# Second block's attention: gates two to a step at first, the dilated projection inside the last steps, weight splits in halves

## The chip, the cores and the metric

The kernel runs on one core of one Trainium2 chip. The metric is the device time of one execution in microseconds (us). Before the change it is 2328.41 us, the median of 3 runs (2326.83 to 2332.44).

## The reference, cut to what matters

Two transformer blocks follow each other, on 256 tokens of width 1024. The change lies in the second block's token mixer, between its input projection and its mixture of experts. There are three dilated groups of four heads (12 in all), and 16 heads with a window of 128 and a sink. Both attentions are projected, each is multiplied by the sigmoid of a gate, and the sum goes through an output projection:

```python
def token_mixer(x, w_in, sinks, w_proj_a, w_proj_b, w_out, slopes):
    h = jnp.einsum('bsd,dc->bsc', x, w_in)
    a_q, a_k, a_v, b_q, b_k, b_v, g_a, g_b = jnp.split(h, SPLIT_POINTS, axis=-1)
    ...
    out_a = dilated_attention(a_q, a_k, a_v, slopes_a)
    out_b = swa_sink_attention(b_q, b_k, b_v, slopes_b, sinks.reshape(SWA_KV_HEADS, SWA_REP))
    merged = (jax.nn.sigmoid(g_a) * jnp.einsum('bsc,cd->bsd', out_a, w_proj_a)
              + jax.nn.sigmoid(g_b) * jnp.einsum('bsc,cd->bsd', out_b, w_proj_b))
    return jnp.einsum('bsd,de->bse', merged, w_out)
```

`out_a` is 256 wide and `out_b` 1024 wide. Then come a layer norm, a router that picks 4 of 32 experts for each token, and the experts, whose weights (12 MB for each) are all read from HBM.

## The kernel before

Each engine runs its own program in order, written as one Python function for each: `pe`, `dve`, `act`, `pool` and `sync` (the queue that issues the weight loads). They meet through semaphores.

**Weights.** A weight tile `t` is loaded by `sync` into one of three raw slots (`t % 3`), after the last use of tile `t - 3` (`wlast[t - 3]`). Matrix products are done in three passes, so the tile is split in two parts of less precision: ScalarE writes the high part in `hi(t, p0, p1)`, piece by piece of 1024 columns, and VectorE subtracts it from the raw tile in `lo(t, p0, p1)`. Before its first piece `hi` waits for the load and for the last use of the tile that held the high slot before (`wlast[hprev[t]]`). A full tile has four pieces, `W_PA` has two. TensorE waits for all pieces of a tile (`s_wlo`, `cum[t + 1]`) before it uses it. `rows(name, ...)` makes one output bank of 128 x 256 with `mm3`, three matmuls for each of 8 contraction slices (24 matmuls; 6 for `pa`, which has two slices).

**Tiles of this part.** `W_GATE` to `W_GATE + 3` are the gates (four output rows of each, so gate row `d` of 0 to 15 needs tile `W_GATE + d // 4`), `W_PA` is the dilated projection, `W_PB` and `W_PB + 1` the window projection, `W_PB + 2` and `W_PB + 3` (the last, `NW - 2` and `NW - 1`) the output projection.

**Banks.** `take` gives the eight PSUM banks in turn, leaving out those that are held, and makes TensorE wait until the bank's earlier content has been emptied. The turn is fixed when the program is built.

**Steps.** The attention is a software pipeline of 15 steps on TensorE. In step s it makes the scores `S2` of head-units 2s and 2s+1 (s below 12), one gate row, the transposes `T2` of the units of step s-2, and the output product of the units of step s-3: `oa` (dilated, steps 3 to 6) or `ob[s - 7]` (window, steps 7 to 14). VectorE in step s takes bias and row maximum of the new scores, divides those of step s-1, and empties `oa` (steps 5, 7) or `ob[s - 8]`; then it runs the split. ScalarE in step s takes the exponentials, the high part of `oa` or `ob[s - 8]`, copies `T2` and the gate row out of PSUM, then runs its side of the split. GpSimd prepares the biases.

Splits stand in steps 1, 5 and 9 (four pieces each: `W_GATE + 1`, `+ 2`, `+ 3`) and in step 12 (`W_PA`). Gate row 15 stands behind the pairs of step 14. After the steps TensorE makes the eight `pa`, then the eight `pb`, then the eight `wx` (output projection, interleaved with the sums of the layer norm). ScalarE takes the two sigmoids after the steps, splits `W_PB`, copies the experts' biases (`bias_`), then `W_PB + 1` and the rest. VectorE multiplies `pa` with the gates, then goes over d from 0 to 7: multiply `pb[d]`, add, subtract the high part of ScalarE (lines 1357, 1359, 1362), with the splits of `W_PB + 1` and `W_PB + 2` before d = 0 and d = 4 and that of `W_PB + 3` behind d = 7.

**The queue.** `sync` waits for the last `ob`, loads the first expert tile, then tile `NW - 2` (behind `pa[7]`), another expert tile, then `NW - 1`, and the other experts as slots come free.

Of the kernel before, what the change touches and what calls it, by code (L numbers as in the profile page):

```python
# [12 lines left out]
ACT = mybir.ActivationFunctionType  # L13
AX = mybir.AxisListType.X
ADD, MULT, SUB, MAX, MIN = ALU.add, ALU.mult, ALU.subtract, ALU.max, ALU.min
# [3 lines left out]
KC = D // P  # L19
L = 256  # L20
# [27 lines left out]
def build(nc, a, out):  # L48
# [154 lines left out]
    W_GATE = W_MIX + 9  # L203
# [52 lines left out]
    def filled(name):  # L256
        return done[name]

    def emptied(name):
        b, n = full[name]  # L260
        return s_free[b], n

    def bank(name):
        return ps[full[name][0]]
# [4 lines left out]
    def freesem(name):  # L269
        return s_free[full[name][0]]  # L270
# [56 lines left out]
    def rows_used(kind, u):  # L327

        if kind == "na":
            return filled(("O", u // 4)) if u % 4 == 3 else (s_no, 3 * (u // 4) + u % 4 + 1)  # L330
        if u >= 8:
            return filled(("ob", (u - 8) // 2))
        return filled(("oa", u // 4)) if u // 2 % 2 else (s_no, 24 + u // 4 + 1)

    def mix_unit(u):

# [37 lines left out]
    def pe(e):  # L374
# [27 lines left out]
        def rows(name, T, t, c, i=0, pair_=None, ready=None, ks=KC):  # L402

            pt = take(e, name)
            w = wpair(t, i)
            for k in range(ks):
                if ready:
                    ready(k)
                r = hpart(k, 0, T) if pair_ is None else half(pair_, slice(None), k)
                ins = mm3(e, pt[:, 0:T], half(w, slice(None), k, slice(P * c, P * c + P)), r, k == 0, k == ks - 1)  # L410
            ins.then_inc(fullsem(name))
# [290 lines left out]
        def gate(i, d):  # L702
            t = W_GATE + 2 * i + d // 4
            if d % 4 == 0:
                e.wait_ge(s_wlo, cum[t + 1])
            rows(("gt", i, d), L, t, d % 4, pair_=xs_)
            wlast[t] = filled(("gt", i, d))


        for step in range(15):  # L710
            if step < 4:
                c, n = step // 2, step % 2
                pts = [take(e, ("S2", 2 * step + z)) for z in range(2)]
                if n == 0:
                    for g in range(3):
                        e.wait_ge(*emptied(("aq", 2 * g + c)))
                        e.wait_ge(*emptied(("ak", 2 * g + c)))
                for g, o, ks in ((0, slice(0, L), slice(0, L)), (1, slice(L, L + P), slice(P * n, P * n + P)),
                                 (2, slice(L + P, L + 2 * P), slice(P * n, P * n + P))):
                    for z, pt in enumerate(pts):  # L720
                        r = slice(64 * z, 64 * z + 64)
                        ins = e.matmul(pt[:, o], aq[r, 2 * g + c, P * n:P * n + P], ak[r, 2 * g + c, ks], start=True,
                                       stop=True)
                        if g == 2:
                            ins.then_inc(fullsem(("S2", 2 * step + z)))
            elif step < 12:
                c = step - 4
                pts = [take(e, ("S2", 2 * step + z)) for z in range(2)]
                if c == 0:
                    for g in range(2):  # L730
                        e.wait_ge(*emptied(("bk", g)))
                e.wait_ge(*emptied(("bq", c)))
                for n, (at, w) in enumerate(((0, P), (P, L))):
                    for z, pt in enumerate(pts):
                        r = slice(64 * z, 64 * z + 64)
                        ins = e.matmul(pt[:, at:at + w], bq[r, c, P * n:P * n + P], bk[r, c // 4, 0:w], start=True,
                                       stop=True)
                        if n:
                            ins.then_inc(fullsem(("S2", 2 * step + z)))
            gate(step // 8, step % 8)  # L740
            if 0 <= step - 2 < 12:
                for u in (2 * step - 4, 2 * step - 3):
                    pt = take(e, ("T2", u))
                    e.wait_ge(s_div, 32 + u + 1)
                    for i, at in enumerate((0, P, 2 * P, 3 * P) if u < 8 else (0, P + 1, 2 * P + 1)):
                        ins = e.transpose(pt[:, P * i:P * i + P], at_[:, u % 6, at:at + P], ident)
                    ins.then_inc(fullsem(("T2", u)))
            if 0 <= step - 3 < 4:
                us = 2 * step - 6, 2 * step - 5
                c, n, jj = mix_unit(us[0])  # L750
                pt = bank(("oa", c)) if n else take(e, ("oa", c), hold=True)
                for u in us:
                    e.wait_ge(*emptied(("T2", u)))
                if us[0] == 0:
                    for i in range(2):
                        for m in range(2):
                            e.wait_ge(*emptied(("av", i, m)))
                for i, (g, kb) in enumerate(((0, 0), (0, 1), (1, n), (2, n))):
                    for z, u in enumerate(us):
                        vh = 64 * (4 * g + jj + z)  # L760
                        ins = e.matmul(pt[64 * z:64 * z + 64, P * n:P * n + P], av[:, kb, vh:vh + 64],
                                       turned_[u % 8][:, P * i:P * i + P], start=i == 0, stop=i == 3)
                ins.then_inc(fullsem(("oa", c)) if n else s_no)
            elif step >= 7:
                c = step - 7
                us = 2 * step - 6, 2 * step - 5
                pt = take(e, ("ob", c))
                for u in us:
                    e.wait_ge(*emptied(("T2", u)))
                if c == 0:  # L770
                    e.wait_ge(*emptied(("bv", 0)))
                    e.wait_ge(*emptied(("bv", 1)))
                vh = 64 * (c // 4)
                for n in range(2):
                    for kb in range(n + 1):
                        for z, u in enumerate(us):
                            i = n + kb
                            ins = e.matmul(pt[64 * z:64 * z + 64, P * n:P * n + P], bv[:, kb, vh:vh + 64],
                                           turned_[u % 8][:, P * i:P * i + P], start=kb == 0, stop=kb == n)
                ins.then_inc(fullsem(("ob", c)))  # L780
            if step in (6, 9):
                held.discard(full["oa", step // 3 - 2][0])
            if step == 14:
                gate(1, 7)


        e.wait_ge(s_wlo, cum[W_PA + 1])
        for d in range(KC):
            rows(("pa", d), L, W_PA, d, pair_=oa_, ks=2,
                 ready=(lambda k: e.wait_ge(*emptied(("oa", k)))) if d == 0 else None)  # L790
        wlast[W_PA] = filled(("pa", KC - 1))
        for i in range(2):
            e.wait_ge(s_wlo, cum[W_PB + i + 1])
            for c in range(4):
# [195 lines left out]
    def dve(e):  # L990
# [298 lines left out]
        for step in range(15):  # L1289
# [41 lines left out]
            if step >= 8:  # L1331
# [1 line left out]
                e.wait_ge(s_ahi, 26 + c + 1)  # L1333
                e.tensor_tensor(straight(ob_[1][:, c, :]), shuffled(bank(("ob", c))[:, 0:L]),
                                straight(ob_[0][:, c, :].bitcast(F32)), SUB).then_inc(freesem(("ob", c)), 1)
            if step in (1, 5, 9):
                lo(W_GATE + 1 + step // 4)
            if step == 12:
                lo(W_PA)
        c = KC - 1  # L1340
        e.wait_ge(s_ahi, 26 + KC)
        e.tensor_tensor(straight(ob_[1][:, c, :]), shuffled(bank(("ob", c))[:, 0:L]), straight(ob_[0][:, c, :].bitcast(F32)),
                        SUB).then_inc(freesem(("ob", c)), 1)


        lo(W_PB)
        e.wait_ge(s_sig, 1)
        for d in range(KC):
            e.wait_ge(*filled(("pa", d)))
            e.tensor_tensor(sg[0][:, d, :], sg[0][:, d, :], bank(("pa", d))[:, 0:L], MULT).then_inc(freesem(("pa", d)), 1)  # L1350
        e.wait_ge(s_sig, 2)
        e.wait_ge(*emptied(("pa", KC - 1)))
        for d in range(KC):
# [248 lines left out]
    def act(e):  # L1602
# [209 lines left out]
        def copied(name, dst, n):  # L1812
            e.wait_ge(*filled(name))
            e.copy(dst, bank(name)[:, 0:n]).then_inc(freesem(name), 1)
# [15 lines left out]
        for step in range(16):  # L1830
# [20 lines left out]
            if 0 <= step - 2 < 12:  # L1851
                for u in (2 * step - 4, 2 * step - 3):
# [1 line left out]
                    e.wait_ge(*filled(("T2", u)))  # L1854
                    w = 4 * P if u < 8 else 3 * P
                    e.copy(turned_[u % 8][:, 0:w], bank(("T2", u))[:, 0:w]).then_inc(freesem(("T2", u)), 1)
            if step < 15:
                copied(("gt", step // 8, step % 8), sg[step // 8][:, step % 8, :], L)
            if step == 14:
                copied(("gt", 1, 7), sg[1][:, 7, :], L)  # L1860
            if step in (1, 5, 9):
                hi(W_GATE + 1 + step // 4)
            if step == 12:
                hi(W_PA)
        for i in range(2):
            e.wait_ge(*emptied(("gt", i, KC - 1)))
            e.activation(sg[i], sg[i], ACT.Sigmoid).then_inc(s_sig, 1)


        hi(W_PB)  # L1870
        for i in range(4):
            e.wait_ge(s_late[i], 16)
        e.wait_ge(*filled(("T2", 23)))
# [349 lines left out]
```

## Time and profile before

| what | value |
|---|---|
| median of 3 runs | 2328.41 us (2326.83 to 2332.44) |
| profiled execution, its own time | 2326.65 us |
| its span | 2324.9 us |
| TensorE busy | 2134.9 us (92%) |
| VectorE busy | 846.8 us (36%) |
| ScalarE busy | 567.4 us (24%) |
| GpSimd busy | 71.8 us (3%) |
| HBM read | 591.03 MB, 255 GB/s over the span |

The busy times are averages over stages with different limits. The attention steps of the second block lie between about 1183.7 and 1270.4 us of the span, `pa` and `pb` up to about 1307 us, and the experts from about 1366 us to the end. In rows of a window the columns are the stretch, then for each engine (PE, PEld, DVE, ACT, POOL) its busy time and count, then PEclk (the granted TensorE clock, 1.00 is full), the DMA share, and GB/s.

### The profile page before, as it was taken

The numbers are of one execution on the slowest core, as the hardware profiler recorded it, in microseconds if no ns is written. First come the engines' busy times: TensorE is split into PE (matmuls) and PEld (weight loads), VectorE is DVE, ScalarE is ACT, GpSimd is POOL, SyncE is SP. The second block draws the span as 40 slices with busy tenths as digits, with TensorE's granted clock in tenths as the row PEclk, the third lists the DMA queues.
The fourth block names the chain that finished last, engine by engine and source line by source line (L and its number), as shares of the span: only waits on it lengthen the run. The fifth ranks groups of instructions, "written<-read, shape, count | busy, mean of one in ns | idle before, by whom it ended". The sixth has DMA issues, their size and how long they took to land.

```text
span 2324.9 us, 27020 instructions
## 1 busy us (share of the span) xinstructions
PE 2134.9 (92%) x11534; PEld 1416.6 (61%) x11534; DVE 846.8 (36%) x1505; ACT 567.4 (24%) x935; POOL 71.8 (3%) x118
## 2 busy tenths in 40 slices
PE   6988999999899998999998879998989988989986
PEld 3766888777677568999987843333333333333332
DVE  4344443352584665765455531111111111111113
ACT  3222332332332434543356230000000000000000
POOL 0000000000000130000031000000000000000000
PEclk8999999999999999999999889999999999999998
DMA  9543343422322454545532559999999999999995
GB/s 353 181 145 109 109 144 110 143 90 93 138 98 75 151 170 137 185 150 185 189 120 103 229 205 411 425 428 427 427 427 428 428 428 428 428 427 428 428 427 210
DMA packets 157229, 593.90 MB, mean 255 GB/s; under 512 B 6416, under 2 KB 79120, under 8 KB 132016
## 3 DMA queue, kind: packets, MB, share of 16 engines
q1 hardware_dynamic: 155104, 589.53, 64.1%
q10 hardware_dynamic: 2000, 2.57, 0.4%
q8 instruction: 94, 1.54, 0.3%
q14 instruction: 31, 0.25, 0.0%
HBM read 591.03 MB, written 1.05 MB: 255 GB/s over the span
## 4 chain that ended last, share of the span: by engine, by line
PE 76%; DMA 13%; DVE 6%; ACT 3%; issue 2%; SPq 1%; ACTq 0%; POOL 0%; DVEq 0%; POOLq 0%
PE ps L897 21%; PE ps L279 13%; PE ps L280 13%; PE ps L281 13%; DMA ring<-in_w_up_dram 12%; PE ps L866 3%; PE ps L883 3%; DVE wr L1004 2%; PE ps L382 2%; PE ps L637 1%; PE ps L616 1%; DMA ring<-in_even_w_in_dram 1%; PE ps L623 1%; SPq L2037 1%; PE ps L396 1%
## 5 line engine op out<-in xcount | busy, mean ns | idle before, releaser
L897 PE MATMUL ps<-ring,big 128*64 128x512 f32 x3072 | 693.4, 607 | 81.3 <-DMA ring<-in_w_up_dram 51.5
L897 PEld LDWEIGHTS ps<-ring,big 128*64 128x64 f32 x3072 | 250.5, 140 | 495.4 <-issue 483.8
L279 PE MATMUL ps<-h_hi,wr 128*128 128x512 f32 (+1 forms) x960 | 341.2, 355 | 29.5 <-DVE h_lo L1056 25.2
L1004 DVE TENSOR_TENSOR wr<-ring,wr 128x1024 fp32r<-128x1024 f32 (+1 forms) x248 | 285.5, 1210 | 140.4 <-ACT wr L1611 140.3
L280 PE MATMUL ps<-h_lo,wr 128*128 128x512 f32 (+1 forms) x960 | 333.2, 347 | 0.0
L281 PE MATMUL ps<-h_hi,wr 128*128 128x512 f32 (+1 forms) x960 | 333.0, 347 | 0.0
L1611 ACT CAST wr<-ring 128x1024 fp32r<-128x1024 f32 (+1 forms) x248 | 238.7, 1032 | 125.6 <-PE ps L281 101.6
L279 PEld LDWEIGHTS ps<-h_hi,wr 128*128 128x128 f32 x960 | 185.3, 193 | 61.6 <-issue 34.9
L280 PEld LDWEIGHTS ps<-h_lo,wr 128*128 128x128 f32 x960 | 185.3, 193 | 23.7 <-issue 2.9
L281 PEld LDWEIGHTS ps<-h_hi,wr 128*128 128x128 f32 x960 | 184.9, 193 | 21.8
L1460 DVE TENSOR_SCALAR hT<-ps 128x512 f32<-128x512 f32 x32 | 20.6, 685 | 258.7 <-PE ps L923 258.7
L1473 DVE TENSOR_SCALAR hT<-ps 128x512 f32<-128x512 f32 x32 | 22.0, 687 | 240.0 <-PE ps L923 240.0
L279 PE MATMUL ps<-x_hi,wr 128*128 128x256 f32 x352 | 104.6, 297 | 1.8 <-DVE x_lo L1272 1.2
L280 PE MATMUL ps<-x_lo,wr 128*128 128x256 f32 x352 | 101.1, 287 | 0.0
L281 PE MATMUL ps<-x_hi,wr 128*128 128x256 f32 x352 | 101.1, 287 | 0.0
L1915 ACT COPY big<-ps 128x512 f32<-128x512 f32 x16 | 9.4, 586 | 371.8 <-PE ps L866 371.8
L1487 DVE COPY xT<-ps 128x512 f32<-128x512 f32 x16 | 11.1, 692 | 221.3 <-PE ps L897 221.3
L1927 ACT ACTIVATE hT<-hT 128x512 f32<-128x512 f32 x32 | 19.6, 630 | 260.5 <-DVE hT L1460 260.5
L279 PEld LDWEIGHTS ps<-x_hi,wr 128*128 128x128 f32 x352 | 69.1, 196 | 6.7 <-issue 4.4
L280 PEld LDWEIGHTS ps<-x_lo,wr 128*128 128x128 f32 x352 | 69.2, 197 | 0.2
L866 PEld LDWEIGHTS ps<-hT,big 128*128 128x128 f32 x512 | 62.3, 199 | 11.5 <-issue 11.5
L281 PEld LDWEIGHTS ps<-x_hi,wr 128*128 128x128 f32 x352 | 69.1, 196 | 0.0
(294 smaller groups left out, 2641.5 us busy)
## 6 DMA issues: line engine op xcount, KB each, us to landing
ring<-in_w_gate_dram SPq DMA_DIRECT2D x64, 2048.0 KB, 22.2
ring<-in_w_up_dram SPq DMA_DIRECT2D x64, 2048.0 KB, 19.7
ring<-in_w_down_dram SPq DMA_DIRECT2D x64, 2048.0 KB, 22.2
ring<-in_ada_w_dram SPq DMA_DIRECT2D x24, 2048.0 KB, 10.6
ring<-in_ffn_w_up_dram SPq DMA_DIRECT2D x44, 1024.0 KB, 7.6
ring<-in_ffn_w_down_dram SPq DMA_DIRECT2D x16, 1408.0 KB, 6.1
ring<-in_w_in_dram SPq DMA_DIRECT2D x9, 2048.0 KB, 7.9
ring<-in_odd_w_qkv_dram SPq DMA_DIRECT2D x6, 2048.0 KB, 8.1
```

The lines of the kernel that those rows point to most:

```text
L279: e.matmul(o, l[0], r[0], start=first, stop=False)
L280: e.matmul(o, l[0], r[1], start=False, stop=False)
L281: return e.matmul(o, l[1], r[0], start=False, stop=last)
L382: ins = e.matmul(pt[32 * g:32 * g + 32, :], s2[:, 2 * g + h, :], wt[:, 2 * g + h, :], start=h == 0, stop=h == 1, skip_group_check=True)
L396: ins = e.matmul(bank(("sq", q))[:, 0:NT[q]], onesd[:, :], part[k % 2][:, 0:NT[q]], start=k == 0, stop=k == KC - 1, skip_group_check=True)
L616: e.matmul(pt[:, :], qT[r0:r0 + 64, c, P * n:P * n + P], kT[r0:r0 + 64, c, :], start=True, stop=True).then_inc(fullsem(("S", u)))
L623: ins = e.transpose(pt[:, P * i:P * i + P], wk[u % 4][:, P * i:P * i + P], ident)
L866: ins = e.matmul(pt[:, P * c:P * c + P], yN[:, n, P * (4 * hf + c):P * (4 * hf + c) + P], Sx[turn_of(b)][:, 0, n, :], start=n == 0, stop=n ...
L883: ins = e.matmul(ps[2 * q + n][:, :], SgT[turn_of(b)][:, P * q:P * q + P], ySB[turn_of(b)][:, n, :], start=False, stop=False, skip_group_c ...
L897: ins = e.matmul(pts[hf][HALF[z], :], lhs[:, k, HALF[z]], wt[:, k % 4, 512 * hf:512 * hf + 512], start=k == 0, stop=False, skip_group_chec ...
L1004: e.tensor_tensor(wr[:, x], ring[:, x], h.bitcast(F32), SUB).then_inc(s_wlo, 1)
L1611: e.copy(wr[:, o], ring[:, SLOT * (t % 3) + 1024 * p:SLOT * (t % 3) + min(1024 * p + 1024, width[t])]).then_inc(s_whi, 1)
```

## The change

`gates_of` gives the gate rows of a step: two each in steps 0 to 2 (rows 0 to 5), one each in steps 3 to 12 (rows 6 to 15), none in 13 and 14. `projections_of` puts `pa[0..3]` into step 13 and `pa[4..7]` into step 14, on TensorE ahead of that step's transposes and output product; VectorE's multiplications of `pa` go into the same steps, behind the split. The sigmoid of the first eight gate rows stands at the end of ScalarE's step 12, the second one at the end of step 13. `split_at` halves the splits: `W_GATE + 1` in steps 0 and 1, `W_GATE + 2` in 3 and 4, `W_GATE + 3` in 6 and 7, `W_PA` in 10, and `W_PB`, which was split after the steps, in 13 and 14. No matmul, copy or load is added or taken away; some wait on other banks, since the order of the takes changes.

```diff
+    def gates_of(step):
+        return (2 * step, 2 * step + 1) if step < 3 else (step + 3,) if step < 13 else ()
+    def projections_of(step):
+        return range(4 * step - 52, 4 * step - 48) if step >= 13 else ()
+    split_at = {0: (W_GATE + 1, 0), 1: (W_GATE + 1, 2), 3: (W_GATE + 2, 0), 4: (W_GATE + 2, 2), 6: (W_GATE + 3, 0),
+                7: (W_GATE + 3, 2), 10: (W_PA, 0), 13: (W_PB, 0), 14: (W_PB, 2)}
...
# TensorE, inside the loop over the steps, between S2 and T2
-            gate(step // 8, step % 8)
+            for d in gates_of(step):
+                gate(d // 8, d % 8)
+            if step == 13:
+                e.wait_ge(s_wlo, cum[W_PA + 1])
+            for d in projections_of(step):
+                rows(("pa", d), L, W_PA, d, pair_=oa_, ks=2,
+                     ready=(lambda k: e.wait_ge(*emptied(("oa", k)))) if d == 0 else None)
+                wlast[W_PA] = filled(("pa", d))
...
-            if step == 14:
-                gate(1, 7)
-        e.wait_ge(s_wlo, cum[W_PA + 1])
-        for d in range(KC):
-            rows(("pa", d), L, W_PA, d, pair_=oa_, ks=2,
...
# VectorE, end of a step
-            if step in (1, 5, 9):
-                lo(W_GATE + 1 + step // 4)
-            if step == 12:
-                lo(W_PA)
+            if step in split_at:
+                t, p = split_at[step]
+                lo(t, p, p + 2)
+            if step == 13:
+                e.wait_ge(s_sig, 1)
+            for d in projections_of(step):
+                e.wait_ge(*filled(("pa", d)))
+                e.tensor_tensor(sg[0][:, d, :], sg[0][:, d, :], bank(("pa", d))[:, 0:L],
+                                MULT).then_inc(freesem(("pa", d)), 1)
...
-        lo(W_PB)
-        e.wait_ge(s_sig, 1)
-        for d in range(KC):
-            e.wait_ge(*filled(("pa", d)))
-            e.tensor_tensor(sg[0][:, d, :], sg[0][:, d, :], bank(("pa", d))[:, 0:L], MULT).then_inc(freesem(("pa", d)), 1)
...
# ScalarE, end of a step
+            for d in gates_of(step):
+                copied(("gt", d // 8, d % 8), sg[d // 8][:, d % 8, :], L)
+            if step in split_at:
+                t, p = split_at[step]
+                hi(t, p, p + 2)
+            if step in (12, 13):
+                i = step - 12
+                e.wait_ge(*emptied(("gt", i, KC - 1)))
+                e.activation(sg[i], sg[i], ACT.Sigmoid).then_inc(s_sig, 1)
...
-        for i in range(2):
-            e.wait_ge(*emptied(("gt", i, KC - 1)))
-            e.activation(sg[i], sg[i], ACT.Sigmoid).then_inc(s_sig, 1)
-        hi(W_PB)
```

## Rows read from the trace of the kernel before

**Rows 1.** Busy times by stretch, the experts in their steady state.
```profile
1600.00:2280.00 680.00, 610.61 (x2814) 257.39 (x2816) 99.14 (x213) 37.43 (x70) 2.90 (x10) 0.98 1.01 428
```

**Rows 2.** Chain of waits in the attention steps: start us, length us, what.
```profile
1183.71 1.08 PE ps L722 x12
...
1187.84 1.08 PE ps L722 x12
...
1208.37 1.02 PE ps L761 x16
...
1231.19 0.66 PE ps L746 x6
1231.84 0.81 PE ps L778 x12
1232.65 0.86 PE ps L736 x8
...
1253.05 0.66 PE ps L746 x6
```

**Rows 3.** TensorE in time: start, length, instruction, [idle before <- releaser].
```profile
754.45 1.09 PE L623 MATMUL ps<-konst,wk 128*128 128x128 f32 x4 [2.98 <-DVE wk L1224]
...
1247.56 0.93 PE L736 MATMUL ps<-big 64*128 64x128 f32 x8 [4.15 <-issue]
...
1282.25 0.55 PE L279 MATMUL ps<-ob_hi,wr 128*128 128x256 f32 x1 [5.98 <-DVE wr L1004]
```

**Rows 4.** TensorE's waits, 1183 to 1375 us: total, times, longest.
```profile
PE ps L736 <- issue: 5.1, 2, 4.2
```

**Rows 5.** Granted clock of short stretches behind idle times.
```profile
754.40:756.40 2.00, 1.95 (x5) 1.22 (x6) 1.49 (x5) 1.26 (x3) 1.14 (x2) 0.50 1.03 400
...
1249.50:1251.50 2.00, 2.00 (x11) 2.00 (x11) 1.89 (x11) 1.97 (x9) 0.00 (x0) 0.50 0.01 4
```

**Rows 6.** VectorE in time, columns as in group 3.
```profile
1193.36 5.67 DVE L1004 TENSOR_TENSOR wr<-ring,wr 128x1024 fp32r<-128x1024 f32 x4 [1.91 <-ACT wr L1611]
...
1239.40 4.64 DVE L1004 TENSOR_TENSOR wr<-ring,wr 128x1024 fp32r<-128x1024 f32 x4 [2.24 <-ACT wr L1611]
1243.94 0.29 DVE L1303 CUSTOM_DVE_ANT_0 at<-ps,ring 128x128 f32<-128x128 f32 x1
...
1247.04 0.42 DVE L1334 TENSOR_TENSOR ob_lo<-ps,ob_hi 128x256 fp32r<-128x256 f32 x1
...
1281.73 2.73 DVE L1350 TENSOR_TENSOR big<-big,ps 128x256 f32<-128x256 f32 x8
...
1289.10 0.41 DVE L1357 TENSOR_TENSOR big<-big,ps 128x256 f32<-128x256 f32 x1
...
1290.86 0.41 DVE L1357 TENSOR_TENSOR big<-big,ps 128x256 f32<-128x256 f32 x1
...
1295.71 0.42 DVE L1357 TENSOR_TENSOR big<-big,ps 128x256 f32<-128x256 f32 x1 [1.04 <-PE ps L281]
```

**Rows 7.** ScalarE in time, columns as in group 3.
```profile
1238.29 3.91 ACT L1611 CAST wr<-ring 128x1024 fp32r<-128x1024 f32 x4
...
1246.65 0.35 ACT L1850 CAST ob_hi<-ps 128x256 fp32r<-128x256 f32 x1
...
1247.65 0.38 ACT L1814 COPY big<-ps 128x256 f32<-128x256 f32 x1
...
1271.21 1.28 ACT L1867 ACT_TABLE_LOAD   x1
1272.51 3.71 ACT L1867 ACTIVATE big<-big 128x2048 f32<-128x2048 f32 x2
...
1279.90 1.04 ACT L1874 CAST bias<-zz 128x1024 fp32r<-128x1024 f32 x1
```

**Rows 8.** The load queue's instructions in time.
```profile
1276.30 0.37 SPq L2031 DMA_DIRECT2D ring<-in_w_out_dram  x1
```

**Rows 9.** Loads issued from 1268 to 1302 us: size, median us to landing.
```profile
ring<-in_w_out_dram SPq DMA_DIRECT2D x2, 2048.0 KB, 11.2
```

More of the change, by code:

```diff
@@ L782, in pe @@
                 held.discard(full["oa", step // 3 - 2][0])
-            if step == 14:
-                gate(1, 7)
-        e.wait_ge(s_wlo, cum[W_PA + 1])
-        for d in range(KC):
-            rows(("pa", d), L, W_PA, d, pair_=oa_, ks=2,
-                 ready=(lambda k: e.wait_ge(*emptied(("oa", k)))) if d == 0 else None)
-        wlast[W_PA] = filled(("pa", KC - 1))
         for i in range(2):
@@ L1856, in act @@
                     e.copy(turned_[u % 8][:, 0:w], bank(("T2", u))[:, 0:w]).then_inc(freesem(("T2", u)), 1)
[L1857 to L1864, printed above, removed]
-        for i in range(2):
-            e.wait_ge(*emptied(("gt", i, KC - 1)))
-            e.activation(sg[i], sg[i], ACT.Sigmoid).then_inc(s_sig, 1)
-        hi(W_PB)
+            for d in gates_of(step):
[7 more added lines that the diff above has]
+                e.activation(sg[i], sg[i], ACT.Sigmoid).then_inc(s_sig, 1)
         for i in range(4):
```

## The prediction

> **What bounds the kernel now.** I first read the busy times by stretch, to know what a microsecond before the experts is worth. In the steady state of the experts the DMA share is 1.01 at 428 GB/s for 680 us [rows 1]: this part runs at the pace of the loads, most of which can only be issued once TensorE frees the slots of the first expert. So whatever moves the start of the experts moves the end by the same amount, and nothing before it is absorbed. Then the chain of waits: from 1183.71 us through all attention steps it lies on TensorE. It gives the prices of a step's parts: dilated scores 1.08, a gate row 3.05 (1187.84 - 1183.71 - 1.08), dilated output 1.02, window transposes 0.66, window output 0.81, window scores 0.86 [rows 2]. A window step is 0.86 + 3.05 + 0.66 + 0.81 = 5.4 us.
>
> TensorE in time shows what the change can win. It stood 4.15 us before the scores of step 11 and 5.98 us before `pb` [rows 3]; with the third wait the score line lost 5.1 [rows 4]. Sum 5.1 + 6.0 = 11.1 us. A long wait also costs clock: behind the one of 4.15 us the granted clock is 0.50, the 1.2 GHz level [rows 5], and scores plus gate took 1253.05 - 1247.56 = 5.49 us instead of 3.91, so 1.6 us more [rows 2, 3].
>
> Why did TensorE wait at step 11? The banks turn, and counting the takes, `S2` of unit 23 gets the bank of `ob[2]`, which VectorE empties at the end of its step 10. VectorE's split of step 9 ran from 1239.40 to 1243.94, its step 10 began only there, and `ob_lo` was done at 1247.46, 0.1 us before TensorE went on [rows 3, 6]. So a split costs because VectorE is in order: what stands behind it is a whole step, whose last instruction frees a bank.
>
> **The change, part by part.** *Constants.* ScalarE's high pieces take 0.98 each (3.91 for four), and VectorE starts 1.11 behind ScalarE (1239.40 - 1238.29) and takes 1.16 a piece [rows 6, 7]. ScalarE begins its split 0.3 us into TensorE's next step. So four pieces end 6.0 us into that step, two pieces 0.3 + 1.1 + 2.3 = 3.8 us into it. VectorE's step behind it takes 3.5 us (1243.94 to 1247.46) [rows 6], and ScalarE has its exponentials behind VectorE's start + 2.7 (1246.65 - 1243.94) [rows 6, 7].
>
> *Work.* The counts of matmuls, copies and loads stay. Moved gates and moved `pa` cost TensorE what they cost now: zero, by themselves. What counts is the waits.
>
> *W_GATE + 1 in steps 0 and 1.* Two gate rows make the steps 1.08 + 2 x 3.05 = 7.2 us: step 1 starts at 1190.9, step 2 at 1198.1. Gate row 4 now stands in step 2 (before: step 4) and wants all four pieces. The last two follow ScalarE's copy of gate row 3 (ready 1198.1): high part from 1198.4, VectorE from 1199.5, done 1201.8. TensorE is there at 1199.2. **New wait 2.7 us**; queued behind it are gate 5 and the first transposes. The split that stands near this place now took 5.67 us instead of 4.64 [rows 6], so up to 1.0 more is possible; I take 0, since VectorE's last two pieces lie later than that one.
>
> *W_GATE + 2 in 3 and 4.* Gate row 8 stands in step 5. In step 3's tail two pieces end 3.4 to 3.8 us into step 4; VectorE takes the scores of step 4 only then, ScalarE's exponentials end 2.7 later (about 6.1), then come transposes and gate copies (ScalarE needs 1247.65 + 0.38 - 1246.65 = 1.4 for such a tail [rows 7], some 0.2 less here without an output bank), so the second half starts at 7.3, its last piece ends 7.3 + 1.1 + 2.3 = 10.7. TensorE's step 4 is 0.86 + 3.05 + about 0.9 + 1.02 = 5.8, and behind the scores of step 5 it is at 6.7. **New wait 4.0**, about 1.6 us of clock behind it.
>
> *W_GATE + 3 in 6 and 7.* Gate row 12 is in step 9, so the tile is in time. The banks are not: the first half ends 3.8 into step 7, the exponentials at 6.5, the tail at 7.9, the second half at 7.9 + 3.4 = 11.3, VectorE's step 8 at 14.8. `S2` of step 9 takes the bank of `ob[0]`, which that step frees last; it is due at 2 x 5.4 = 10.8. **Wait 4.1**, in the place of the 4.15 before. Two halves in neighbouring steps add up, since the second begins late by what the first delayed.
>
> *W_PA in 10:* two pieces delay VectorE's step 11 to 7.3 us; that step frees `ob[3]` for transposes that come 8.4 us behind: hidden, with 1.1 us to spare. Without that cover a wait of about 2 us would stand in step 12 (7.3 - 5.4).
>
> *Steps 13 and 14.* From the start of step 13: four `pa` (24 matmuls, as many as a gate row) 2.9, transposes 0.66, `ob[5 + 1]` 0.81, `pa[4]` 0.7: at 5.1 TensorE wants the bank of `pa[0]`. ScalarE: copies until 0.3, table load 1.3, half of the sigmoids 1.86 (3.71 / 2) [rows 7] to 3.4, high part of `ob[5]` 3.8, copies 4.5, first piece of `W_PB` 5.5; VectorE two pieces to 7.9, then `pa[0]` x gate 0.34 (2.73 / 8) [rows 6]: 8.2. **New wait 3.2**, 1.6 of clock behind it. Then `pa[5..7]` and `ob[7]`, 3.0 + 1.6. The second half of `W_PB` ends at about 12.2, TensorE is ready for `pb` at 5.1 + 3.2 + 4.6 = 12.9: **the wait of 5.98 goes away**.
>
> *Sum to the start of `pb`.* Waits 2.7 + 4.0 + 4.1 + 3.2 = 14.0 against 11.1: +2.9. Clock before that point: 3 x 1.6 against one: +3.2. The idle of 2.98 us has half clock behind it [rows 3, 5]; 2.7 is just under it, and I charge it nothing (0 or 1.6 for the range). `pb` starts at 1282.25 + 6.1 = 1288.4.
>
> *From there.* VectorE's loop decides. Before, its fourth multiplication started 13.5 us behind `pb` (1295.71), having waited 1.04 for TensorE [rows 6], which had run `pb` at half clock first. Now that part is spared, but the copy of the biases (1.04) [rows 7] and the high part of `W_PB + 1` come only behind `ob[7]`: 0.4 + 1.0 + 1.1, four pieces 4.6, three rounds of 1290.86 - 1289.10 = 1.76 [rows 6]: 12.4. So the fourth round is at 1300.8, 5.1 us late, and all later splits, the layer norm, the router and the first expert hang on it. Sum on the profiled execution's own time: 2326.65 + 5.1 = 2331.8; the median of the runs is 1.8 higher than that execution: 2333.5 us.
>
> *A table load* is moved, not added. Sigmoid's load takes 1.28 and the sigmoid starts 0.02 behind it [rows 7]. The Trainium skill (ScalarE: Activation LUTs, What ACT_TABLE_LOAD costs) counts a drain of 1.38 us on top. By that the wait in step 14 would be 1.4 longer and the sum +6.5; the trace does not show such a drain here, and I go by the row.
>
> **The rivals.** *A, the forecast:* the waits are as above, +2 to +7.
>
> *B, slower: the output projection's first tile lands late.* Its issue stood at 1276.30 [rows 8], 20 us ahead of its use; now it is issued at `ob[7]`, behind an expert tile, and is wanted 12.4 + 1.2 = 13.6 us later. Two MB at 428 GB/s [rows 1] are 4.9 us; in order it lands about 1.5 + 9.8 = 11.3 behind, as the 11.2 of now [rows 9] says. If it shares the engines with the second expert tile issued right behind it, that is 16.2: 2.6 late, +7.7, 2336.1. It decides from 13.6 on.
>
> *C, faster: the halves hide.* If ScalarE and VectorE slip the halves into their gaps, the 11.1 us and two clock falls (3.2) go: -14.3, 2314.1; half of it still gives -7. Against it: the arithmetic of the banks, and the gate rows that follow their tile by one step. For it: VectorE idles a third of each step.
>
> *D, nothing:* waits only move, the clock doesn't fall behind the shorter ones: -2 to +2, 2328.4.
>
> **Numbers.** 0.3% (7.0 us) is about what a measurement of this kernel can tell from no change. A 0.50 (a tenth of it above +7), D 0.20, B 0.15, C 0.12, other delays 0.03. Faster 0.12; slower 0.15 + 0.05 + 0.03 = 0.23, and 0.04 for the 1.6 of clock behind the first wait on top: 0.27; same 0.61. A's own range is 2330 to 2336. The range 2323 to 2341 leaves out most of C below and a twentieth above.
>
> **What would show it.** In the changed profile: TensorE waits near 1199 (2.7), at gate row 8 (4.0), at `S2` of step 9 (about 4) and at `pa[5]` (3.2), no wait before `pb`; VectorE's fourth round near 1301; the experts 5 us later, their pace the same. Wrong would be: a gate row that finds its tile ready in step 5, no wait in step 9, a clock that stays at 1.00, or a high part of the output tile that waits on a DMA.

## The result, and the profile after

| | before | after |
|---|---|---|
| median of 9 runs | 2330.34 us (2326.02 to 2332.44) | 2334.35 us (2331.99 to 2341.63) |
| profiled execution, its span | 2324.9 us | 2334.0 us |

The ratio is 1.0023, with a 95% interval of 1.0012 to 1.0034: 2.8 to 7.9 us slower. That is clear of no change, though less than the 0.3% that the prediction takes as just measurable, and close to the forecast of 2333.5. The profiled spans differ by 9.1 us, more than the runs. The profiled execution of before took 2326.65 us, 3.7 under its kernel's median; that of after took 2335.82, 1.5 over its own. So I read the difference by stretches and take only the stretch that the change touches. One execution of e6 below took 5816 us; it counts as slow, and the ratios are of the fast runs.

Busy times from the first scores of the attention steps to the first `pb`, first of the kernel before, then of the changed one. The columns are the stretch, its length, then PE, PEld, DVE, ACT and POOL busy, the granted clock, the DMA share and GB/s.

```profile
1183.71:1282.25 98.54, 87.22 (x785) 78.80 (x785) 59.20 (x190) 65.00 (x156) 31.52 (x46) 0.97 0.32 119
```

```profile
1186.00:1291.70 105.70, 92.48 (x786) 84.03 (x785) 60.55 (x195) 62.46 (x152) 29.65 (x46) 0.92 0.25 91
...
1600.00:2280.00 680.00, 612.37 (x2823) 257.37 (x2820) 99.88 (x214) 37.93 (x70) 2.92 (x10) 0.98 1.01 428
```

The stretch grew by 7.2 us. TensorE's work is the same, but it stood 105.70 - 92.48 = 13.2 us instead of 98.54 - 87.22 = 11.3 (+1.9), and was busy 5.3 us longer with it, at a mean clock of 0.92 instead of 0.97. The last row answers to [rows 1]: the experts run at the same pace as before, so what is lost ahead of them stays lost.

Where it stood, from TensorE in time of the changed kernel; these rows answer to [rows 3]:

```profile
1204.11 0.58 PE L279 MATMUL ps<-x_hi,wr 128*128 128x256 f32 x1 [2.94 <-DVE wr L1016]
...
1230.29 0.58 PE L279 MATMUL ps<-x_hi,wr 128*128 128x256 f32 x1 [4.08 <-DVE wr L1016]
...
1256.75 0.93 PE L748 MATMUL ps<-big 64*128 64x128 f32 x8 [3.56 <-DVE ob_lo L1346]
...
1287.08 0.39 PE L279 MATMUL ps<-oa_hi,wr 128*128 128x256 f32 x1 [2.64 <-DVE big L1355]
...
1326.08 1.22 PE L814 MATMUL ps<-xT,onesd 128*128 128x256 f32 x2 [4.54 <-DVE xT L1383]
```

The first two are gate rows 4 and 8, which wait for VectorE's split of their tile. The third is `S2` of step 9, which waits for the bank of `ob[0]`; the fourth is `pa[5]`, which waits for the bank of `pa[0]`. Between that and `pb` (1291.70) nothing waits any more: the 5.98 us of before are gone. The last is the wait of the layer norm, which was there before. All four before `pb` are within 0.6 us of the forecast (2.7, 4.0, 4.1, 3.2).

The clock behind those waits, to be read beside [rows 5]; the granted clock is the number behind the five engines' columns:

```profile
1206.10:1208.10 2.00, 2.00 (x11) 2.00 (x11) 0.37 (x1) 0.13 (x2) 0.00 (x0) 0.50 0.54 196
...
1230.30:1232.30 2.00, 2.00 (x9) 2.00 (x10) 1.89 (x13) 1.21 (x6) 0.00 (x0) 0.51 0.00 0
1256.70:1258.70 2.00, 1.95 (x13) 1.62 (x14) 0.86 (x6) 0.56 (x2) 0.00 (x0) 0.73 1.01 386
```

From `pb` on VectorE sets the pace. Its rows in time, which answer to those from 1281.73 on in [rows 6]:

```profile
1294.21 4.63 DVE L1016 TENSOR_TENSOR wr<-ring,wr 128x1024 fp32r<-128x1024 f32 x4 [1.57 <-ACT wr L1623]
1298.76 0.41 DVE L1369 TENSOR_TENSOR big<-big,ps 128x256 f32<-128x256 f32 x1
...
1304.04 0.41 DVE L1369 TENSOR_TENSOR big<-big,ps 128x256 f32<-128x256 f32 x1
```

The fourth round starts at 1304.04, 12.3 us behind `pb` (forecast 12.4), and VectorE no longer waits for TensorE in front of it (1.04 before, [rows 6]). Counted from the first scores that is 118.0 us instead of 112.0: +6.0. The matmuls that gather the first expert's tokens start 187.7 us behind the first scores instead of 181.9: +5.8, which fits the ratio (1.0023 is 5.4 us). Of the 9.1 us between the spans the rest lies outside: 2.3 ahead of the attention and 1.0 in the experts, where nothing was changed.

### The profile page after: what moved, and what is told of

It reads as the page before. It is cut to its first block, busy times and chain, and to the rows that moved or that the text cites. A ratio compares the mean times of both kernels' runs of the same rounds, so it can differ in the third digit from the quotient of the medians.

```text
span 2334.0 us, 27020 instructions
## 1 busy us (share of the span) xinstructions
PE 2140.1 (92%) x11534; PEld 1418.4 (61%) x11534; DVE 847.2 (36%) x1505; ACT 567.4 (24%) x935; POOL 69.6 (3%) x118
## 3 DMA queue, kind: packets, MB, share of 16 engines
HBM read 591.03 MB, written 1.05 MB: 254 GB/s over the span
## 4 chain that ended last, share of the span: by engine, by line
PE 75%; DMA 12%; DVE 6%; ACT 4%; issue 1%; SPq 1%; ACTq 0%; POOL 0%; DVEq 0%; POOLq 0%
PE ps L909 21%; PE ps L279 13%; PE ps L280 13%; PE ps L281 13%; DMA ring<-in_w_up_dram 11%; DVE wr L1016 3%; PE ps L878 3%; PE ps L895 2%; PE ps L394 2%; PE ps L649 1%; PE ps L628 1%; DMA ring<-in_even_w_in_dram 1%; ACT wr L1623 1%; PE ps L635 1%; SPq L2046 1%
## 5 line engine op out<-in xcount | busy, mean ns | idle before, releaser
L280 PE MATMUL ps<-f_lo,wr 128*128 128x512 f32 x176 | 68.6, 390 | 0.0
```

Of the source, the lines that this page charges most:

```text
L280: e.matmul(o, l[0], r[1], start=False, stop=False)
```

## The experiments

In the table "stretch" is the time from the first scores to the first `pb`, "stood" is that less TensorE's busy time, and "expert" is the time from the first scores to the gather of the first expert. All are of one profiled execution each; the ratios are of several runs each against the kernel before, run beside it.

| kernel | stretch | busy | stood | expert | ratio (95%) |
|---|---|---|---|---|---|
| before | 98.5 | 87.2 | 11.3 | 181.9 | 1 |
| changed | 105.7 | 92.5 | 13.2 | 187.7 | 1.0023 (1.0012 to 1.0034) |
| e1 | 101.9 | 91.6 | 10.3 | 187.2 | 1.0015 (1.0006 to 1.0024) |
| e2 | 99.4 | 89.8 | 9.5 | 182.7 | 1.0008 (0.9999 to 1.0017) |
| e3 | 102.2 | 90.9 | 11.3 | 187.1 | 1.0006 (0.9997 to 1.0015) |
| e4 | 100.7 | 94.1 | 6.6 | 183.8 | 1.0013 (1.0004 to 1.0022) |
| e5 | 106.4 | 89.7 | 16.7 | 190.0 | 1.0036 (1.0023 to 1.0050) |
| e6 | 105.5 | 90.9 | 14.6 | 188.9 | 1.0028 (1.0018 to 1.0037) |
| e7 | 93.0 | 88.4 | 4.6 | 175.1 | 0.9977 (0.9967 to 0.9986) |
| e8 | 92.9 | 88.4 | 4.5 | 175.3 | 0.9967 (0.9956 to 0.9979) |
| e9 | 104.8 | 91.3 | 13.5 | 187.3 | 1.0031 (1.0019 to 1.0043) |

One execution says these times to within a microsecond or two only, because the clock behind a wait differs from one to the next. Gate row 4 waits 2.94 us in the changed kernel, e2, e3, e5, e6 and e9, with the same code up to there; gate rows 4 and 5 then took 8.4 us in the changed kernel and e3 and 8.5 in e6, but 7.3 in e2, e5 and e9, against 5.9 at full clock (e1 and e7). Behind `pb`, from the first sums of the layer norm to the gather, no edit changes anything, and it took 47.6 to 49.2 us. So "expert" is the rougher column of the two. No ratio of e1 to e6 or e9 is clear of that of the changed kernel: their intervals overlap. What these runs show is which wait comes or goes, and by how much; only e7 and e8 differ from the changed kernel in their ratio as well.

The theory is that of the prediction: each wait has its own cause, a tile that is split too late or a bank that VectorE frees last, and the clock behind a wait is a cost of its own. The rivals are that VectorE's load as a whole bounds the steps, so that a wait that is taken away comes back; and that only the waits count.

**e1: the first gate tile ahead of the steps.** ScalarE and VectorE split `W_GATE + 1` before the first scores.

```diff
-    split_at = {0: (W_GATE + 1, 0), 1: (W_GATE + 1, 2), 3: (W_GATE + 2, 0), ...
+    split_at = {3: (W_GATE + 2, 0), ...
# VectorE, behind the last bq; ScalarE: hi(W_GATE + 1) ahead of the copies of bk
+        lo(W_GATE + 1)
```

> The changed kernel, with the whole split of W_GATE + 1 moved ahead of the steps, where ScalarE and VectorE had idle time, instead of in halves in steps 0 and 1. Waits-and-clock theory: gate row 4 finds its tile ready, so the wait of 2.9 us in step 2 and the 2.5 us of half clock behind it go; the other three waits of the steps stay. From the first scores to the first pb 5.4 us less than in the changed kernel, and the ratio to the kernel before falls from 1.0023 to about 1.0000. Rival (VectorE's total load bounds the steps, so a wait that goes comes back later): the stretch stays within 1 us, ratio about 1.002.

```profile
1183.35:1285.25 101.90, 91.62 (x786) 82.93 (x785) 55.58 (x190) 58.80 (x148) 28.21 (x46) 0.92 0.27 94
```

The wait in step 2 is gone and no other one came: TensorE stood 2.9 us less, exactly that wait. But its busy time fell by 0.9 only, not by 2.5: the mean clock is 0.92 as in the changed kernel, since more of the work behind the other waits ran at the low level (gate row 8 took 5.3 us behind its wait of 4.08, and 4.5 in the changed kernel). And a new wait appeared behind `pb`, on ScalarE's high part for the output projection (ScalarE in time):

```profile
1300.57 1.05 ACT L1623 CAST wr<-ring 128x1024 fp32r<-128x1024 f32 x1 [1.66 <-DMA ring<-in_w_out_dram]
```

That is rival B of the prediction, a load that lands late. It did not bite in the changed kernel (12.6 us from issue at 1292.20 to landing, its first use at 1305.25), but it had about half a microsecond to spare. ScalarE wants the tile 13.1 us behind its issue in both kernels; what differs is the load, which took 14.7 us here. Why it took longer isn't shown. The ratio moved a third as far as expected, and its interval holds that of the changed kernel's 1.0023. At the expert 0.5 us is left of the 3.8: the late tile took 1.7, and the layer norm and the router, which no edit touches, took 1.5 more than in the changed kernel's execution.

**e2: the second gate tile one step earlier.**

```diff
-    ... 3: (W_GATE + 2, 0), 4: (W_GATE + 2, 2), ...
+    ... 2: (W_GATE + 2, 0), 3: (W_GATE + 2, 2), ...
```

> The changed kernel, with the two halves of the split of W_GATE + 2 in steps 2 and 3 instead of 3 and 4. Waits-and-clock theory: gate row 8 in step 5 finds its tile ready; 4.1 us of wait and 1.5 us of half clock go, and nothing new comes, since the banks of steps 3 and 4 are freed early enough: 5.6 us less up to the first pb, ratio about 0.9999. Rival (the splits' place does not matter, only their sum): within 1 us, ratio about 1.002.

```profile
1188.16:1287.53 99.37, 89.83 (x786) 81.32 (x785) 59.51 (x192) 62.40 (x154) 30.52 (x46) 0.95 0.28 96
```

The stretch is 6.3 us shorter (expected 5.6): 3.7 less of standing (the 4.1 gone, and 0.4 new in front of `pb`) and 2.7 less busy. Of the 2.7, gate row 8 gives 1.5; the rest is clock behind the three other waits, where nothing was edited (1.0 less at gate row 4, 1.3 more at `S2` of step 9, 1.4 less at `pa[5]`). The same splits one step earlier brought no new wait in the steps. The rival that only the sum of the splits matters is out. The ratio is 1.0008 and not the expected 0.9999, which its interval only just takes in.

**e3: the halves of the third gate tile apart.**

```diff
-    ... 6: (W_GATE + 3, 0), 7: (W_GATE + 3, 2), ...
+    ... 5: (W_GATE + 3, 0), 7: (W_GATE + 3, 2), ...
```

> The changed kernel, with the halves of the split of W_GATE + 3 in steps 5 and 7 instead of 6 and 7. Theory that neighbouring halves add up: the second half now begins on time, so VectorE's step 8 ends 7.3 us behind the start of TensorE's step 8 and not 9.4; the wait at the scores of step 9 falls from 3.6 to about 1.9 us, and with so short a wait the clock stays full (1.5 us more): 1.7 to 3.2 us less, ratio about 1.0013. Rival (only the last half counts, as it alone stands before the bank that is needed): the wait stays at 3.6, ratio 1.0023. Other outcome: four pieces' worth of delay anywhere costs the same, 0.

TensorE in time, at the scores of step 9, and the clock of the 2 us behind it:

```profile
1252.02 0.93 PE L748 MATMUL ps<-big 64*128 64x128 f32 x8 [1.60 <-DVE ob_lo L1346]
```

```profile
1252.00:1254.00 2.00, 1.98 (x17) 1.65 (x18) 0.89 (x6) 0.47 (x2) 0.00 (x0) 1.00 1.02 396
```

The wait is 1.6 instead of 3.6, and the clock stays full. Two halves in neighbouring steps do add up, and apart they do not. The stretch fell by 3.5 us; at the expert only 0.6 is left in this execution, again with ScalarE waiting for the output projection's tile (1.3 us; the load took 14.3) and with 1.6 us more in the layer norm and the router, while the runs as a whole are 1.0006.

**e4: TensorE busy while it waits.**

```diff
-            if d % 4 == 0:
-                e.wait_ge(s_wlo, cum[t + 1])
-            rows(("gt", i, d), L, t, d % 4, pair_=xs_)
+            spare = {W_GATE + 1: 24, W_GATE + 2: 33}.get(t, 0)
+            def first(k):
+                if k == 0 and d % 4 == 0:
+                    for _ in range(spare):
+                        e.matmul(bank(("gt", i, d))[:, 0:L], xs_[0][:, 0, 0:P], xs_[0][:, 0, :], start=True, stop=True)
+                    e.wait_ge(s_wlo, cum[t + 1])
+            rows(("gt", i, d), L, t, d % 4, pair_=xs_, ready=first)
```

> The changed kernel; TensorE fills its waits for the tiles of gate rows 4 and 8 with 24 and 33 matmuls (128 x 256) into the bank that the row is going to overwrite, so that it waits no shorter but is not idle. If the clock is a cost of its own: granted clock 1.00 in both gate rows, 2.5 and 1.5 us less, 4.0 in all, ratio about 1.0006. If only the waits count, or the rows behind a wait are slow for another reason: 0, ratio 1.0023.

The waits of TensorE in the stretch (total, times, longest), and the clock behind the spare matmuls of gate row 8:

```profile
PE ps L754 <- DVE ob_lo L1352: 3.6, 1, 3.6
PE ps L279 <- DVE big L1361: 2.6, 1, 2.6
PE ps L279 <- DVE wr L1022: 0.4, 1, 0.4
```

```profile
1225.30:1228.30 3.00, 3.00 (x26) 3.00 (x26) 2.81 (x17) 2.12 (x9) 0.00 (x0) 1.00 0.00 0
```

The stretch is 5.0 us shorter (expected 4.0). Up to `S2` of step 9, where the 57 matmuls that nobody needs act, it is 4.0: gate rows 4 and 5 took 5.9 us instead of 8.4, gate row 8 3.0 instead of 4.5. The last microsecond came behind `pa[5]`, where nothing was edited and the clock happened to stay full. Nothing was split earlier; only the clock stayed full. So the clock is a cost of its own, and the rival that only the waits count is out.

**e5: `W_PB` split behind the steps, as before.**

```diff
-    ... 10: (W_PA, 0), 13: (W_PB, 0), 14: (W_PB, 2)}
+    ... 10: (W_PA, 0)}
# VectorE and ScalarE, behind the steps
+        lo(W_PB)
+        hi(W_PB)
```

> The changed kernel with the split of W_PB put back whole behind the steps. It frees VectorE for pa in step 13, so the wait at pa[5] (2.6 us) should go, and a wait before the first pb of about 6 us should come back. By the ledger of the prediction pb starts 2.6 us later, the fourth round of VectorE's loop 3.3 us later: ratio to the kernel before about 1.0037. Rival (taking W_PB's split into the steps wins the whole 6 us that the kernel before waited there): 6 us later, 1.0049. Second rival (the wait at pa[5] eats all of it): no difference, 1.0023.

```profile
1294.06 0.58 PE L279 MATMUL ps<-ob_hi,wr 128*128 128x256 f32 x1 [6.08 <-DVE wr L1016]
```

The wait of 6 us is back, that at `pa[5]` is gone. `pb` starts only 0.7 us later than in the changed kernel (expected 2.6); 1.0 of the difference to the forecast is the cheaper clock behind gate row 4. VectorE's fourth round is 2.3 us later (expected 3.3), because `pb` now begins at half clock and VectorE waits 1.0 us for TensorE before each of its later rounds. The first expert comes 2.2 us later. The ratio of 1.0036 is the expected one, but its interval overlaps that of the changed kernel. So the last part of the change looks like a gain of two or three microseconds, not of the six that stood there: part of it is paid at `pa[5]`.

**e6: VectorE multiplies `pa` before it splits.**

```diff
# VectorE, end of a step: the block "for d in projections_of(step)" moved ahead of
             if step in split_at:
                 t, p = split_at[step]
                 lo(t, p, p + 2)
```

> The changed kernel with VectorE's multiplications of pa ahead of the halves of W_PB's split in steps 13 and 14. The wait at pa[5] goes (2.6 us and 0.7 of clock). Theory that VectorE's split, not TensorE, then sets the start of pb: the second half ends only about 0.3 us earlier, TensorE waits for it instead, and pb starts at most 1 us earlier; ratio about 1.002. Rival (the wait at pa[5] counts in full): 3.3 us less, ratio 1.0009.

```profile
1293.34 0.38 PE L279 MATMUL ps<-ob_hi,wr 128*128 128x256 f32 x1 [4.02 <-DVE wr L1016]
```

The wait at `pa[5]` has moved in front of `pb`, as 4.0 us, and the start of `pb` is where it was (105.5 against 105.7). Here VectorE's split sets that start. It ends 0.8 us later than in the changed kernel, not 0.3 earlier as expected, since the multiplications now stand ahead of it. In the changed kernel it ended 1.05 us before `pb`, and TensorE, slowed behind `pa[5]`, came last; so VectorE is the next limit close behind. The long wait also puts the beginning of `pb` at half clock, and the first expert is 1.2 us later. The interval of the ratio overlaps that of the changed kernel.

**e7: the edits of e1, e2 and e3 together.**

```diff
+    split_at = {2: (W_GATE + 2, 0), 3: (W_GATE + 2, 2), 5: (W_GATE + 3, 0),
+                7: (W_GATE + 3, 2), 10: (W_PA, 0), 13: (W_PB, 0), 14: (W_PB, 2)}
```

> The changed kernel with the three edits of the runs before together: W_GATE + 1 whole ahead of the steps, the halves of W_GATE + 2 in steps 2 and 3, those of W_GATE + 3 in steps 5 and 7. If the waits are independent, those of steps 2 and 5 are gone and that of step 9 is 1.6: from the first scores to the first pb some 14 us less than in the changed kernel (105.7 there), so about 92, and, with the 1.7 us that ScalarE loses to the late output-projection tile, about 12 less at the end: ratio about 0.997. If VectorE's load bounds the steps: new waits in steps 6 to 9, at most 6 us less, ratio about 1.000.

```profile
1183.63:1276.59 92.96, 88.41 (x785) 79.94 (x784) 55.45 (x191) 58.04 (x148) 28.15 (x46) 0.96 0.29 103
```

The stretch is 93.0 us, 12.7 less than in the changed kernel and 5.6 less than before, and no new wait came. It is 1.3 short of the expected 14, because the wait at `S2` of step 9 is 1.92 us and not 1.6, and behind it the clock did fall: up to `pa[5]` TensorE took 1.5 us more than in e3. The runs are faster than the kernel before (ratio 0.9977, the interval all below 1, though this too is less than 0.3%). VectorE was busy only 55 of 93 us: its load as a whole never was the bound.

**e8: and the output projection's load ahead of the expert's.**

```diff
+        w(NW - 2)
         e.wait_ge(*filled(("ob", KC - 1)))
         expert(0)
-        w(NW - 2)
```

> The run before plus one edit of the load queue: the first output-projection tile is issued ahead of the first expert tile. In the changed kernel it lands 12.5 us behind its issue, just in time; where pb starts without half clock in front of it, ScalarE waited 1.7 us (idle in the trace) for it. If that is the next limit: no wait of ScalarE on a DMA before its second split of the output projection, 1.7 us less than the run before, ratio about 0.9962. Rival (the expert tile is now late, or another wait takes its place): 0.

```profile
1280.48 0.37 SPq L2041 DMA_DIRECT2D ring<-in_w_out_dram  x1
1281.54 1.64 SPq L2107 DMA_DIRECT2D ring<-in_w_gate_dram  x2
```

The tile is issued 1.1 us ahead of the expert tiles now, and the expert tiles are in time. But in the profiled execution of e7 ScalarE had not waited for that tile, so there was nothing to win in it: 175.3 us to the expert against 175.1. The tile had taken 12.7 us there and was wanted 13.1 behind its issue; in the changed kernel and in e1 to e7 and e9 it took 12.4 to 14.7. Issued first, it took 8.7. The ratio is 0.9967, and its interval overlaps that of e7. That this edit wins a microsecond over many runs isn't shown. It is the fastest version that was run.

**e9: the third gate tile in one piece.**

```diff
-    ... 6: (W_GATE + 3, 0), 7: (W_GATE + 3, 2), ...
+    ... 7: (W_GATE + 3, 0), ...      # lo and hi take p to p + 4 for this tile
```

> The changed kernel with the split of W_GATE + 3 in one piece in step 7 instead of in halves in steps 6 and 7. Ledger: four pieces end 6.0 us into TensorE's step 8, VectorE's step 8 takes 3.5 more and frees the bank that the scores of step 9 want at 9.5, due at 5.4: a wait of about 4.1 us instead of 3.6, same clock, so at most 0.6 us more than the changed kernel, ratio about 1.0025. If halving was worth what a hidden half would be (the wait doubles with four pieces): a wait of 6 us or more, ratio about 1.0035.

```profile
1254.77 0.49 PE L747 MATMUL ps<-big 64*128 64x128 f32 x4 [3.81 <-DVE ob_lo L1345]
```

A whole tile in step 7 costs 3.8 us of waiting, two halves in 6 and 7 cost 3.6. Halving by itself bought 0.2 us. The stretch even came out 0.9 us shorter, since the clock cost 1.0 less behind gate row 4. The ratio, 1.0031, does not tell e9 from the changed kernel.

## Why the prediction was right, point by point

- **What it is worth.** The experts run at 428 GB/s in both kernels, and the 6 us that were lost ahead of them are in the ratio. Right.
- **Four waits.** Forecast 2.7, 4.0, 4.1 and 3.2, measured 2.94, 4.08, 3.56 and 2.64. Sum 13.2 against the forecast 14.0, so +1.9 over before instead of +2.9. The causes were as named: e1 and e2 took the tile waits away singly, e3 showed the bank and the adding up of neighbouring halves, e9 that a whole tile costs nearly the same (3.8). The third was one subtraction off on paper: 14.8 - 10.8 is 4.0, not 4.1.
- **The clock: the term that was mis-sized.** The prediction charged three falls of 1.6 us and none behind the wait of step 2, +3.2 over before. Measured +5.3: two gate rows behind the 2.94 us wait took 8.4 us instead of 5.9, so 2.5 where 0 was charged; the three falls that it did charge cost 1.4 to 1.5 each. The 2.5 is itself a draw, as the same wait cost 1.5 in e2, e5 and e9. The two errors, -1.0 and +2.1, make the start of `pb` 7.2 us late instead of 6.1. That they partly cancel is luck.
- **From `pb` on.** 12.3 us to VectorE's fourth round, forecast 12.4. Right; so +6.0 there against the forecast 5.1.
- **The number.** 2333.5 against 2334.35 looks closer than it is: the forecast added 5.1 to a median of 3 runs, and over 9 runs that median is 1.9 us higher. As a difference, +5.1 stands against +4.0 by the medians and +5.4 by the ratio, which is good enough.
- **The table load.** It took 1.28 us in the changed kernel too, began 0.03 us behind the copy before it, and the sigmoid began 0.01 behind it. The drain of 1.38 us that the Trainium skill (ScalarE: Activation LUTs, What ACT_TABLE_LOAD costs) adds is not in this trace either.
- **Rival B**, the late tile, did not decide the changed kernel's profiled execution, but was nearer than its chance said: the tile had half a microsecond to spare, and in e1, e2, e3 and e9 ScalarE waited for it (1.7, 0.6, 1.3 and 0.3 us). The forecast of 11.3 us to landing was short: it took 12.6, and up to 14.7 in e1.
- **Rival C**, hidden halves, fell because of where the halves stand, not because of their number: e7 hides almost all of them.

## What to carry to other kernels

When work is spread over the steps of a software pipeline, count for each piece who needs it and what stands behind it in its engine's order. Here a piece that was consumed one step later was late, and pieces in neighbouring steps added up; the same pieces one step earlier cost no wait (e2), and a step apart they cost 1.6 us instead of 3.6 (e3). On TensorE a short wait can cost nearly as much again in clock as in time, so a wait that is removed wins more than its length. And a change that moves a load closer to its use should leave room for the load's spread: with the queue's order of the changed kernel the same tile took 12.4 to 14.7 us, and was wanted at 13.1.

## What the hardware showed beyond that

The same work behind nearly the same wait ran at three speeds. The 18 matmuls of `pa[5..7]` followed a wait of 2.6 us in all three of these kernels; the rows are about their stretches in e2, in the changed kernel and in e7 (the last two take in the start of `ob[7]`):

```profile
1283.89:1286.10 2.21, 2.21 (x18) 2.21 (x18) 2.21 (x5) 2.14 (x3) 0.00 (x0) 1.00 0.00 0
```

```profile
1287.08:1290.29 3.21, 3.21 (x20) 2.99 (x22) 3.21 (x6) 2.13 (x3) 0.00 (x0) 0.70 0.00 0
```

```profile
1271.94:1275.80 3.86, 3.86 (x20) 3.63 (x20) 3.86 (x8) 2.13 (x3) 0.00 (x0) 0.56 0.00 0
```

The clock was at its full level, fell from it during the work, or was mostly at the low one: up to the first matmul of `ob[7]` 2.35, 3.14 and 3.85 us. Up to `pb` the last two come out alike again, 1.4 us more than e2's time without its wait. In the changed kernel it fell after the work had been going for more than a microsecond, as the chain of waits shows (start, length):

```profile
1287.08 0.39 PE ps L279
...
1288.30 0.12 PE ps L281
1288.42 0.16 PE ps L279
1288.58 0.21 PE ps L280
```

From 0.12 to 0.21 us a matmul is the step from 2.4 to 1.2 GHz. So the price of a wait of 2 to 4 us is a range, over the executions of these kernels: nothing behind 1.60 (e3), 1.5 behind 1.92 (e7 and e8), 0 to 1.4 behind 2.64, 1.5 to 2.6 behind 2.94, 1.5 to 2.8 behind 3.56 and 1.4 to 2.3 behind 4.08. A forecast should carry that as a range for each wait and not as one number.
